# Gathering one tile further ahead, and one loop instead of two, in the expert stage of a decoder layer

## The reference

```
logits = xn @ w_router + b_router;  top_v, top_i = top_k(logits, 4);  gates = softmax(top_v)
for each of the chosen experts e of a token:
    hmid = xn @ w_up[e] + b_up[e]                       # 1024 -> 2048
    act  = min(hmid[:1024], 7) * sigmoid(1.702 * min(hmid[:1024], 7)) * (clip(hmid[1024:], -7, 7) + 1)
    y   += gate * (act @ w_down[e] + b_down[e])         # 1024 -> 1024
```

## Time and profile before

| | us |
|---|---|
| median of 3 runs | 1566.41 |
| lowest and highest | 1562.13, 1570.34 |
| span of the profiled execution | 1565.7 |
| busy: PE, its weight loads, DVE, ACT, POOL | 1300.1, 697.0, 530.9, 209.8, 225.4 |
| DMA in the whole span | 480.52 MB, 307 GB/s |

### The profile page before, as it was taken

How to read it: one execution, slowest core, us unless ns; L and a number is a source line. 1 busy time by engine, 2 the same in 40 slices (tenths; PEclk the granted TensorE clock), 3 DMA queues, 4 the chain that set the end, 5 groups by cost and what they waited for, 6 DMA issues and landing times.

```text
span 1565.7 us, 30929 instructions
## 1 busy us (share of the span) xinstructions
PE 1300.1 (83%) x11087; PEld 697.0 (45%) x11088; DVE 530.9 (34%) x1344; ACT 209.8 (13%) x561; POOL 225.4 (14%) x349
## 2 busy tenths in 40 slices
PE   7999999999898977669998996695796886857865
PEld 5778777778786532223443332231232332312322
DVE  2999756643573251111211111111111111111155
ACT  2111232414240210000000000000000000000001
POOL 2008700124220010000100000000010000001320
PEclk9999999999999998779999997898898998978987
DMA  7586455204037789999978999999999999999996
GB/s 186 125 267 158 101 128 143 86 9 109 1 119 230 279 364 419 420 410 416 419 290 357 405 417 418 419 419 416 419 419 417 406 390 412 418 417 419 418 372 237
DMA packets 147329, 480.52 MB, mean 307 GB/s; under 512 B 15438, under 2 KB 76118, under 8 KB 114471
## 3 DMA queue, kind: packets, MB, share of 16 engines
q1 hardware_dynamic: 135695, 463.37, 77.3%
q0 software_dynamic: 2560, 10.29, 1.6%
q10 hardware_dynamic: 9024, 6.17, 1.2%
HBM read 462.42 MB, written 18.21 MB: 307 GB/s over the span
## 4 chain that ended last, share of the span: by engine, by line
PE 59%; DMA 17%; DVE 8%; issue 6%; SPq 3%; POOL 3%; ACT 2%; DVEq 1%; POOLq 0%
PE bank L1287 17%; DMA arena<-in_w_up 16%; PE bank L1299 10%; PE bank L782 9%; PE bank L1255 5%; PE bank L1273 3%; DVE acc L1826 3%; PE bank L1174 2%; PE bank L1182 2%; PE bank L865 2%; POOL acc L548 2%; SPq L447 2%; SPq L450 1%; PE bank L1082 1%; POOL temps L545 1%
## 5 line engine op out<-in xcount | busy, mean ns | idle before, releaser
L1287 PE MATMUL bank<-arena,gate 128*32 128x512 f32 x3264 | 420.0, 643 | 125.4 <-DMA arena<-in_w_up 124.8
L1287 PEld LDWEIGHTS bank<-arena,gate 128*32 128x32 f32 x3264 | 103.9, 113 | 395.8 <-issue 270.7
L782 PE MATMUL bank<-arena 128*128 128x304 f32 (+1 forms) x1024 | 263.9, 420 | 3.7 <-DMA arena<-in_w_in 2.2
L2368 DVE COPY gate<-bank 128x256 f32<-128x256 f32 x46 | 19.6, 425 | 634.9 <-PE bank L1299 634.9
L782 PEld LDWEIGHTS bank<-arena 128*128 128x128 f32 x1024 | 196.9, 193 | 68.2 <-ACT zs L1497 3.1
L1299 PE MATMUL bank<-arena,gate 128*32 128x256 f32 x3264 | 190.5, 384 | 30.9 <-ACT gate L1717 29.3
L1299 PEld LDWEIGHTS bank<-arena,gate 128*32 128x32 f32 x3264 | 112.4, 111 | 96.7 <-issue 27.1
L1826 DVE SCALAR_TENSOR_TENSOR acc<-arena,pcol,acc x240 | 126.3, 609 | 0.1
L672 POOL TENSOR_TENSOR qkv<-qkv 128x192 f32<-128x192 f32 x46 | 29.4, 639 | 613.3 <-DVE qkv L2312 613.3
L1273 PE MATMUL bank<-qkv 128*128 128x512 f32 x102 | 59.5, 666 | 49.9 <-DVE gate L2354 23.4
L1255 PE MATMUL bank<-qkv 128*32 128x256 f32 (+1 forms) x1224 | 87.2, 401 | 2.0 <-POOL qkv L675 1.2
(11 more groups left out here) (424 smaller groups left out, 1169.7 us busy)
## 6 DMA issues: line engine op xcount, KB each, us to landing
arena<-in_w_up SPq DMA_DIRECT2D x256, 1024.0 KB, 12.7
arena<-in_w_down SPq DMA_DIRECT2D x256, 512.0 KB, 8.6
arena<-in_w_in SPq DMA_DIRECT2D x32, 1024.0 KB, 10.4
y_d<-gate ACTq DMA_DIRECT2D x188, 32.0 KB, 4.9
y_d<-gate POOLq DMA_DIRECT2D x1, 4608.0 KB, 28.3
arena<-in_w_conf_out SPq DMA_DIRECT2D x4, 1024.0 KB, 5.1
arena<-in_state_dn_S SPq DMA_DIRECT2D x8, 512.0 KB, 7.3
arena<-in_w_dn_out SPq DMA_DIRECT2D x1, 4096.0 KB, 15.2
```

What stands on the lines that cost most here:

```text
L782: last = mm(bank[2 * (j % 2) + f][:, 0:cols.stop - cols.start], wring[:, slot, k, P * half:P * (half + 1)], rhs[:, k, cols], start=(k == 0 ...
L1287: last = mm(hidden(q)[v], xgT[:, i, SL * q0:SL * (q0 + 1)], parts(wup[k], q)[v], start=False, stop=(k == KC - 1), skip_group_check=True)
```

## The change

Four things are changed together.

1. In a tile step the gather moves from the middle to the end and is for tile b+2 instead of b+1. The turn of the gathered rows moves from the end to the middle, behind the turn of the activations and ahead of down, with a new wait on `y_ready`, because it now writes the second half of bank 6, whose first half holds the result of down. ACT's order becomes `copy_actt`, `store_y`, `sigmoid`, `copy_xg(b+2)`.
2. Tiles 2 to 15 are written out on PE, ACT, DVE and POOL instead of running in a loop.
3. The two nested loops with two copies of the step become one loop of `SLOTS = 48` rounds with one conditional step. The table now has one number for each round: 0 for a round without a tile, else the tile number less 15.
4. The last four tiles and the start follow the new order.

```diff
-        info_i = small(O_MID + MID, I32)
+        info_i = small(O_MID + SLOTS, I32)
+        xgt_bank = bank[6][:, W:2 * W]
...
                 up_bias(b)
                 up(b, range(0, 4), now_in)
-                gather(b + 1)
                 turn(act_h, bank[4], s["act_ready"], b, s["actt_done"])
+                if not first(prev):
+                    pe.wait_ge(s["y_ready"], prev)
+                turn(xg, xgt_bank, s["xg_copied"], b + 2, s["xgt_done"])
                 down(prev, range(KC), prev_in)
                 up(b, range(4, KC), now_in)
-                turn(xg, bank[0][:, W:2 * W], s["xg_copied"], b + 2, s["xgt_done"])
+                gather(b + 2)
...
-            with pe.Fori(2, HEAD) as b:
+            for b in range(2, HEAD):
                 tile_step(b)
             turn_gates()
             pe.wait_ge(s["mask_ready"], 3)
             nx = pe.value_load(info_i[0:1, 0:1], min_val=0, max_val=XB)
-            with pe.Fori(0, MID) as i:
-                b = pe.value_load(info_i[0:1, bass.ds(i + O_MID, 1)], min_val=0, max_val=XB + MID) + HEAD
-                tile_step(b)
-                with pe.Fori(0, EXTRA) as j:
-                    with pe.If(i + j * MID < nx):
-                        tile_step(b + j + 1)
+            with pe.Fori(0, SLOTS) as m:
+                nth = pe.value_load(info_i[0:1, bass.ds(m + O_MID, 1)], min_val=0, max_val=XB + MID)
+                with pe.If(nth > 0):
+                    b = nth + (HEAD - 1)
+                    tile_step(b)
...
                 up(b, range(0, 4), now_in)
-                if i < LAST - 1:
-                    gather(b + 1)
                 turn_choice(i)
                 turn(act_h, bank[4], s["act_ready"], b, s["actt_done"])
+                if i < LAST - 1:
+                    pe.wait_ge(s["y_ready"], prev)
+                    turn(xg, xgt_bank, s["xg_copied"], b + 2, s["xgt_done"])
                 down(prev, range(KC), prev_in)
...
-                if i < LAST - 1:
-                    turn(xg, bank[0][:, W:2 * W], s["xg_copied"], b + 2, s["xgt_done"])
+                if i < LAST - 2:
+                    gather(b + 2)
...
             def tile_step(b):
-                copy_xg(b + 1)
                 copy_actt(b - 1)
+                store_y(b - 1)
                 sigmoid(b)
-                store_y(b - 1)
+                copy_xg(b + 2)
```

More of the change, by code:

```diff
@@ L48 @@
 EXTRA = -(-XB // MID)
+SLOTS = MID * (1 + EXTRA)
 O_MID = 1 + NT + NE
@@ L281, in build @@
         thr = temps[:, 2456:2457]
-        info = temps[0:1, 2464:2464 + O_MID + MID]
-        extra = temps[0:1, 2464 + O_MID + MID:2464 + O_MID + (1 + EXTRA) * MID].rearrange("p (i j) -> p i j", j=EXTRA)
+        info = temps[0:1, 2464:2464 + O_MID + SLOTS]
+        rank, runs = (temps[0:1, 2464 + O_MID + SLOTS * i:2464 + O_MID + SLOTS * (i + 1)] for i in (1, 2))
         tcmp = zs[:, :, :].rearrange("p k n -> p (k n)")[:, 0:(NT + 1) * NE].rearrange("p (t e) -> p t e", e=NE)
@@ L705, in _ @@
             selected(1)
-            with pool.Fori(2, HEAD) as b:
+            for b in range(2, HEAD):
                 choose(b)
@@ L709, in _ @@
             nx = pool.value_load(info_i[0:1, 0:1], min_val=0, max_val=XB)
[L710 to L717, removed]
+            with pool.Fori(0, SLOTS) as m:
+                nth = pool.value_load(info_i[0:1, bass.ds(m + O_MID, 1)], min_val=0, max_val=XB + MID)
+                with pool.If(nth > 0):
+                    b = nth + (HEAD - 1)
+                    choose(b)
+                    selected(b)
             for i in range(3):
@@ L1366, in _ @@
             gather(0)
-            turn(xg, bank[0][:, W:2 * W], s["xg_copied"], 1, s["xgt_done"])
+            turn(xg, xgt_bank, s["xg_copied"], 1, s["xgt_done"])
             up_bias(0)
@@ L1371, in _ @@
             up(0, range(4, KC), 16)
-            turn(xg, bank[0][:, W:2 * W], s["xg_copied"], 2, s["xgt_done"])
+            turn(xg, xgt_bank, s["xg_copied"], 2, s["xgt_done"])
             pe.wait_ge(s["tab_ready"], 1)
-            tile_step(1)
-            with pe.Fori(2, HEAD) as b:
+            in1 = landed_for(1)
+            up_bias(1)
+            up(1, range(0, 4), in1)
+            gather(2)
+            turn(act_h, bank[4], s["act_ready"], 1, s["actt_done"])
+            down(0, range(KC), 16)
+            up(1, range(4, KC), in1)
+            pe.wait_ge(s["y_ready"], 1)
+            turn(xg, xgt_bank, s["xg_copied"], 3, s["xgt_done"])
+            gather(3)
+            for b in range(2, HEAD):
                 tile_step(b)
@@ L1737, in _ @@
             sigmoid(0)
-            tile_step(1)
-            with act.Fori(2, HEAD) as b:
+            copy_xg(2)
+            copy_actt(0)
+            store_y(0)
+            sigmoid(1)
+            copy_xg(3)
+            for b in range(2, HEAD):
                 tile_step(b)
             nx = act.value_load(info_i[0:1, 0:1], min_val=0, max_val=XB)
[L1742 to L1747, removed]
+            with act.Fori(0, SLOTS) as m:
+                nth = act.value_load(info_i[0:1, bass.ds(m + O_MID, 1)], min_val=0, max_val=XB + MID)
+                with act.If(nth > 0):
+                    b = nth + (HEAD - 1)
+                    tile_step(b)
             for i in range(LAST):
                 b = nx + (NE - LAST + i)
-                if i < LAST - 1:
-                    copy_xg(b + 1)
                 act.wait_ge(s["pgt_done"], i + 2)
@@ L1754, in _ @@
                 copy_actt(nx + (NE - LAST + i - 1))
-                sigmoid(b)
                 if i == 0:
                     store_y(nx + (NE - LAST - 1))
+                sigmoid(b)
+                if i < LAST - 2:
+                    copy_xg(b + 2)
             copy_actt(nx + (NE - 1))
@@ L2292, in copy_xgt @@
                 v.tensor_tensor(xgT.rearrange("p j (q n) -> p j q n", q=G),
-                                bank[0][:, W:2 * W].rearrange("p (j q n) -> p j q n", j=W // P, q=G),
+                                xgt_bank.rearrange("p (j q n) -> p j q n", j=W // P, q=G),
                                 pcol[:, :, R_NF:R_NF + 1].rearrange("p (q j) o -> p j q o", j=W // P)
@@ L2323, in _ @@
             v.tensor_scalar(selcol[:, 1:NT + 1], etab[:, 1:NT + 1], ecol, None, ALU.is_equal)
-            for j in range(EXTRA):
-                last = v.tensor_scalar(extra[:, :, j], iota_t[0:1, 0:MID], 0.0, None, ALU.mult)
+            for j in range(1 + EXTRA):
+                last = v.tensor_scalar(rank.rearrange("p (i j) -> p i j", i=MID)[:, :, j], iota_t[0:1, 0:MID],
+                                       info[:, 0:1], float(MID * (j - 1)), ALU.subtract, ALU.add)
             then(last)
[L2327 to L2334, removed]
+            then(v.tensor_scalar(rank, rank, 0.0, None, ALU.is_lt))
+            then(v.tensor_tensor_scan(runs, rank, ones[0:1, 0:SLOTS], -1.0, ALU.add, ALU.add))
+            then(v.tensor_tensor(runs, runs, iota_t[0:1, 0:SLOTS], ALU.subtract))
+            then(v.tensor_tensor(info[:, O_MID:O_MID + SLOTS], runs, rank, ALU.mult))
+            v.tensor_copy(info_i[0:1, O_MID:O_MID + SLOTS], info[:, O_MID:O_MID + SLOTS])
             then(v.tensor_scalar(info[:, 1:1 + NT], etab[0:1, 0:NT], 16.0, 16.0, ALU.mult, ALU.add))
@@ L2377, in _ @@
             tile_step(1)
-            with dve.Fori(2, HEAD) as b:
+            for b in range(2, HEAD):
                 tile_step(b)
@@ L2382, in _ @@
             nx = dve.value_load(info_i[0:1, 0:1], min_val=0, max_val=XB)
[L2383 to L2388, removed]
+            with dve.Fori(0, SLOTS) as m:
+                nth = dve.value_load(info_i[0:1, bass.ds(m + O_MID, 1)], min_val=0, max_val=XB + MID)
+                with dve.If(nth > 0):
+                    b = nth + (HEAD - 1)
+                    tile_step(b)
             def add_tile(i, c, out):
```

## The result

The change made the kernel slower. Four runs of it have a median of 1599.3 us (1590.9 to 1612.5), the kernel before 1564.3 in the same comparison; the ratio is 1.0211, 95% interval 1.0175 to 1.0247, so +33 us, where -4.2 was forecast and 1574 was the upper end. The four runs differ by 1.3% among themselves; all of them, and those of the kernel before, are in the same state.

The account below looks back on a forecast made before the run. Weight DMA was taken to bound experts of one or two tiles, PE only those of three. Terms -2.3 (three-tile expert), -0.5 (loop) and -1.4 (last four tiles) sum to -4.2 from 1566.4: 1562.2 us, range 1552 to 1574.

Parts of the forecast that it names:

- two of them 30.8 against 30.7 of DMA: hidden: Single loop: with register work of 0.7 us a plain round, 1.5 with a skip, two steps stay hidden under DMA.
- -0.5: Single loop's term in us: only the dry stretch near 1250 counts, bounds -3.4 and +4.
- rival (b): No change, by register work in written-out steps and loop rounds (plain 1 us, skips 2.1): +0.5, 1567 us; chance 0.15.
- The gather of tile 50 moves from the middle of step 49 to the end of step 48, where PE waits for DVE anyway: Last four tiles: down starts earlier and frees weights SP waits for, -1.4 us, bounds -4 and +3.
- Match on DVE and choice on POOL keep their order, so 0: Tile step: the gather's choice matrix is ready in time, 1.0 us to spare, so no cost.
- rival (d): Gather at the step's end waits for POOL; a delay of 1.8 us takes the 0.78 back: 1566 us; chance 0.05.
- The 2.3 count in full: Three-tile expert, tiles 12 to 15: the issue in tile 16's step comes 2.3 us earlier, DMA being dry ahead of it.
- the +0.64 of an end: End of a tile step: the gather's 1.47 us covers the 0.83 wait for DVE and sticks out by 0.64.
- Its last slice lands at 794.48 whatever PE does: Tile 12, first of the three-tile expert: DMA was full until there, so the landing time does not depend on PE.
- The switch: From written-out part to loop, ahead of tile 16: 3.29 us of issue and the slow 2.07 bias were taken to stay.
- rival (c): Faster: at the switch the 3.29 and slow bias go, near 1250 the gather keeps PE going: -11, 1555.5 us; chance 0.18.
- rival (a): Slower: late code stops three or four of fourteen written-out steps, 4 to 7 us each: +8 to +16, 1570 to 1578; chance 0.17.

Follow-up runs that it names:

- match: The changed kernel with DVE's match operation moved up, right behind the copy of down's result, in the last four tiles; 1585.1 us, ratio 1.0110.
- both: The changed kernel with the two nested loops and their table taken back and DVE's match operation moved up in the last tiles; 1564.9 us, ratio 0.9995.
- nested: The changed kernel with its single loop taken back to the two nested loops and their table on all four engines; 1576.7 us, ratio 1.0081.
- dyn: The changed kernel with DVE's match operation moved up and the 48 rounds replaced by a register-bound loop over working tiles only; 1556.2 us, ratio 0.9946.
- order_only: The kernel before with only the new step order and DVE's match operation moved up; tiles 2 to 15 and nested loops as before; 1567.3 us, ratio 1.0018.
- early: The changed kernel with DVE's match operation moved up, a register-bound loop over working tiles, gate table and nx load ahead of tile 2; 1554.4 us, ratio 0.9921.
- head_only: The kernel before with nothing but tiles 2 to 15 written out on the four engines; 1568.7 us, ratio 1.0019.
- noload: The changed kernel with DVE's match operation moved up and 47 constant rounds under a condition on the round's number, no number loaded; 1570.0 us, ratio 1.0032.

## Why the prediction was wrong

**The step that failed first: "two of them 30.8 against 30.7 of DMA: hidden".** The mechanism (register work shows after the gather) was seen and its bounds were 0 and 2.1 us a round, but the value was set by the row with work queued: 0.7 and 1.5, where 1.42 and 2.82 were measured. (Its own terms, unrounded, make 14.34 + 0.7 + 14.34 + 1.5 = 30.9.) That row belongs to a bias that stands behind 0.44 us of transposes and a wait for DVE of which the pause is a part; behind a gather no such cover is left. With the measured values alone two tiles make 2 x (14.0 + 1.42) = 30.8 us and with a skip 32.2, 1.5 more than the DMA wants, so by this estimate the loop would have lost several us. **The rest is the clock**, which the sum had nowhere: steps took 17.1 us, and 18.5 with a skip, instead of 15.4 and 16.8. How the 22.5 us divide between pauses and clock is read from these rows; no run holds the clock up with the pauses left in. The rows for it were there: a bias of 2.07 us behind a pause at the switch and near 1250. I took them as two single events and not as what every pause of that length may do. In all -0.5 was said and +22.5 came in the trace (20.3 between match and both); rival (b) had the mechanism, at 1 us a plain round, and priced it at 1567.

**"The gather of tile 50 moves from the middle of step 49 to the end of step 48, where PE waits for DVE anyway", -1.4.** Wrong in sign as the change stood, by the order on DVE: "Match on DVE and choice on POOL keep their order, so 0" was read on a step of the loop, 1.0 us to spare, and not on `last_step`, whose match stands elsewhere. It was rival (d), at another place, and cost 12 to 16 us (both against nested, match against the changed kernel) instead of the delay of 1.8 that I gave it. Once match is moved, this part is far better than forecast: from tile 48's issue to the output the kernel before takes 94.4 us and the version called both 88.6. Part of it is that PE no longer waits 2.17 us for DVE ahead of a sum, as it did at 1493.40 in the kernel before; the rest was not taken apart.

**"The 2.3 count in full".** The steps were even better than predicted: 13.99 us written out, for 14.34. But the issue in tile 16's step came 0.3 us earlier, in both 0.5 later. Timeline of PE in the changed kernel, the end of tile 8's step, which in the kernel before ran without a wait:

```profile
731.93 1.07 PE L1288 MATMUL bank<-arena,gate 128*32 128x512 f32 x8 [0.17 <-DMA arena<-in_w_up]
735.00 1.43 PE L1288 MATMUL bank<-arena,gate 128*32 128x512 f32 x8 [2.00 <-DMA arena<-in_w_up]
736.19 2.94 PE L1256 MATMUL bank<-qkv 128*32 128x256 f32 x24
739.06 1.12 PE L1274 MATMUL bank<-qkv 128*128 128x512 f32 x2
```

A faster PE comes to the last slice early and waits 2.00 us for it; then the clock falls, and the gather behind takes 2.94 us for 1.6. The next bias is at 739.06 where it was at 735.98. But the slow gather is not what costs the gain: in nested, match, both and dyn it takes 1.61 us at this place, and their bias still comes at 736.8 to 737.4, by the time from the start of tile 0 0.5 to 0.8 us later than in the kernel before. What all kernels of the new order share is that the gather now stands between the last slice and the next expert's first matmuls, the +0.64 of an end, which I counted from tile 12 on and not for the experts before it. So "Its last slice lands at 794.48 whatever PE does" was the step that failed here: tile 12's last slice was used at 796.40 in the changed kernel, and at 795.2 in order_only, which has the new order and no written-out step. From the start of tile 0 the issue in tile 14's step comes 1.0 us later in order_only than before (260.8 and 259.8) and 1.3 later in the changed kernel. From that slice to the issue in tile 16's step it is 53.9 us for 56.2, so 2.2 of the 2.3 did come, but 1.9 had been lost before. That they were lost by the gather's place is argued from these rows, not tried.

**The switch** stayed nearly as predicted (4.01 us of pause in the timeline for 4.85, bias at 2.07 as before), and early shows that it was worth 3.1 us up to the bias and 4.2 up to the issue: rival (c)'s size there, but only by another edit.

**Code that comes late (rival (a), 0.17).** Its stops were not found: 16 to 17 more packets and no idle time of PE without a releaser in tiles 2 to 15; head_only is 0.2% slower (0.03 to 0.35), so a small cost is not excluded. In the loop, from 862 to 1473 us, with all its 17 skips, the changed kernel has no packet of instructions at all, so by the trace its pauses are no fetches. The Trainium skill (Runtime: NRT & Kernel Launch, Instruction fetch mechanics) says that a taken branch out of the window of two pages fetches its target by DMA; this trace doesn't bear that out for PE's loop.

## What to carry to other kernels

Ask of a loop's jump, condition and register loads what stands right in front of them: they are free ahead of a wait and cost 0.5 to 1.4 us a round behind back-to-back matmuls, and behind pauses of 1.4 us the clock fell in a part of the steps. Give a loop a bound in a register rather than empty rounds under a condition (1599.3, 1585.1 with match moved, 1556.2 with the bound); alone, in the old order, the bound gave 0.1% by the medians. When a stage is bound by DMA, ask of every reordering what now stands between the last slice of one expert and the first of the next. When an operation is moved to an earlier point, follow what it needs in every copy of the step, the ones written out for the last tiles above all.

## What the runs showed of the hardware that was not expected

- PE's register work behind a gather: 0.53 us for jump and two loads (dyn), 0.78 with a condition (noload), 1.42 with a number read from the table for the condition (changed kernel); an empty round 0.73 us in noload and 1.42 in the changed kernel.
- It adds up, 1.40 to 1.44, 2.80 to 2.87 and 4.23 to 4.26 us for one, two and three rounds, whether or not PE had waited for a slice in that step; only the first and the last round of the loop differ (1.49 and 3.23).
- Beside POOL's indirect DMAs PE gets its matmuls in lots of 4 or 5 every 1.4 us, in the changed kernel in the down of tile 47 as before in the up of tile 48; the timeline of the changed kernel:

```profile
1507.57 0.64 PE L1300 MATMUL bank<-arena,gate 128*32 128x256 f32 x5 [0.34 <-issue]
...
1508.99 0.66 PE L1300 MATMUL bank<-arena,gate 128*32 128x256 f32 x4 [0.78 <-issue]
...
1510.41 1.08 PE L1300 MATMUL bank<-arena,gate 128*32 128x256 f32 x5 [0.75 <-issue]
```

  POOL issues its eight indirect DMAs from 1500.48 to 1510.32. The pause of 3.92 us of the earlier trace rows lies beside them too, in the kernel before; that is its place and not a cause, and it was not tried.
